# A sparse-attention stage whose two heads of a pair are normalised by one multiplication, with score buffers ordered by job

## What is computed

```
p_cmp = softmax(sc - slope * dist_c)
p_slc = softmax(ss - slope * dist_s)
p_win = softmax(sw - slope * dist_w)
o = gb[..., 0:1] * o_cmp + gb[..., 1:2] * o_slc + gb[..., 2:3] * o_win
```

## Time and profile before

| | |
|---|---|
| median of three runs | 3542.05 us (3542.04 to 3548.92) |
| the profiled execution | 3543.41 us |
| its span | 3541.6 us |
| the sparse attention's stretch in it | 1065.7 to 1337.0 us |

### The profile page before, as it was taken

One profiled execution on the slowest core, in us unless ns is written; L12 is line 12 of the kernel. 1 busy time (PEld: TensorE's weight loads), 2 busy tenths in 40 slices (PEclk: granted clock), 3 DMA queues, 4 the chain that ended last, 5 costly groups with the idle time before them and its releaser, 6 DMA issues.

```text
span 3541.6 us, 43801 instructions
## 1 busy us (share of the span) xinstructions
PE 3417.5 (96%) x16665; PEld 2705.3 (76%) x16665; DVE 1998.2 (56%) x4683; ACT 708.1 (20%) x1739; POOL 83.3 (2%) x104
## 2 busy tenths in 40 slices
PE   8999999999999999999998989999999999999988
PEld 3487688888655678888887767888887888887766
DVE  4473476544305667765456568543464667557566
ACT  2221021100114441211001153022112011131143
POOL 0000000000000000000000100000000000000100
PEclk9999999999999999999999999999999999999999
DMA  3202212222311112122221311212211222102311
GB/s 144 95 25 84 83 48 84 95 83 84 119 36 37 49 49 84 48 90 90 84 88 67 102 42 48 84 60 84 72 58 59 99 74 84 37 25 96 102 42 48
DMA packets 40120, 255.16 MB, mean 72 GB/s; under 512 B 5812, under 2 KB 5940, under 8 KB 11632
## 3 DMA queue, kind: packets, MB, share of 16 engines
q1 hardware_dynamic: 31616, 224.41, 17.8%
q0 software_dynamic: 3808, 16.12, 1.3%
q10 hardware_dynamic: 4496, 11.89, 1.2%
HBM read 243.73 MB, written 2.18 MB: 69 GB/s over the span
## 4 chain that ended last, share of the span: by engine, by line
PE 89%; DVE 8%; issue 1%; ACT 1%; DMA 1%; ACTq 0%; POOL 0%; POOLq 0%; DVEq 0%
PE PL L1194 27%; PE PX L1194 20%; PE PL L884 14%; PE PL L1535 4%; PE PL L1382 3%; PE PX L1644 2%; DVE SCR L2965 2%; PE PL L863 1%; PE PL L860 1%; PE PL L1298 1%; PE PX L1318 1%; DVE SCR L2980 1%; PE PL L1560 1%; PE PL L1347 1%; PE PX L894 1%
## 5 line engine op out<-in xcount | busy, mean ns | idle before, releaser
L884 PE MATMUL PL<-xn,ring 128*128 128x264 f32 (+1 forms) x1600 | 501.4, 471 | 11.6 <-DVE xn L2338 11.1
L884 PEld LDWEIGHTS PL<-xn,ring 128*128 128x128 f32 x1600 | 304.1, 192 | 193.9 <-issue 162.2
L1194 PE MATMUL PL<-Z,ring 128*128 128x256 f32 (+1 forms) x1344 | 318.1, 387 | 10.4 <-DVE Z L3355 8.6
L1194 PEld LDWEIGHTS PL<-Z,ring 128*128 128x128 f32 x1344 | 258.8, 193 | 52.3 <-DVE Z L3355 9.7
L1194 PE MATMUL PL<-AUX,ring 128*128 128x256 f32 (+1 forms) x1088 | 251.5, 379 | 0.0
L2381 DVE TENSOR_TENSOR Z<-PL,SCR 128x512 f32<-128x512 f32 (+1 forms) x72 | 50.2, 698 | 352.1 <-PE PL L884 337.2
L1194 PEld LDWEIGHTS PL<-AUX,ring 128*128 128x128 f32 x1088 | 206.6, 190 | 28.5 <-DVE AUX L2701 0.2
L1194 PE MATMUL PL<-xn,ring 128*128 128x264 f32 (+1 forms) x736 | 174.5, 389 | 12.7 <-DVE xn L2338 11.5
L1194 PE MATMUL PX<-Z,AUX 128*128 128x264 f32 (+1 forms) x768 | 178.3, 383 | 2.7 <-DVE Z L3163 2.7
L1194 PEld LDWEIGHTS PL<-xn,ring 128*128 128x128 f32 x736 | 141.1, 192 | 38.1 <-issue 10.9
L1813 ACT ACTIVATE SCR<-PL 128x256 f32<-128x256 f32 (+1 forms) x72 | 27.6, 383 | 698.7 <-PE PL L1194 698.7
(11 more groups left out here) (520 smaller groups left out, 5965.3 us busy)
## 6 DMA issues: line engine op xcount, KB each, us to landing
ring<-w_tiles SPq DMA_DIRECT2D x212, 1024.0 KB, 4.8
Z<-Z ACTq DMA_DIRECT2D x16, 264.0 KB, 4.7
SCR<-head_rows POOLq DMA_DIRECT2D x16, 264.0 KB, 3.8
AUX<-norm_scratch POOLq DMA_DIRECT2D x8, 528.0 KB, 6.5
Z<-mem POOLq DMA_DIRECT2D x3, 1024.0 KB, 11.0
cst<-consts ACTq DMA_DIRECT2D x1, 2188.5 KB, 15.9
resid<-x ACTq DMA_DIRECT2D x4, 512.0 KB, 9.6
Z<-norm_scratch POOLq DMA_DIRECT2D x4, 512.0 KB, 8.1
```

The costliest lines, as they stand in the source:

```text
L884: mm = pe.matmul(PL[:, 2 * h + c, 0:e - a], ring[t % 2][:, k, P * h:P * h + P], src_block(name, k)[:, a:e], start=k == 0, stop=k == KB - 1)
L1194: mm = pe.matmul(ps, lhs(k), rhs(k), start=kc == 0 and k == 0, stop=kc == per - 1 and k == 3)
```

## The change

The score buffers are counted by job, not by entry of the list: job number m has buffer m % 4 and the small columns of that buffer, so that the two heads of a pair lie in buffers 0 and 1, or 2 and 3. The compressed scores get columns of their own (5280 to 5536 of the scratch tile). At the first head of a pair normalise returns at once. At the second head it waits for that head's exponentials and does both heads: one reciprocal of the two sums, one product with the two gates, and one multiplication of both heads' columns by the two factors, spread along the columns. That raises na_nrm by two. The waits of the other functions are as before.

```
+        def nsa_scores(n):
+            return SCR[:, 5280:5536] if NSA[n][0] == "cmp" else Sbuf[NSA_JOB[n] % 4]
...
-                            mm = pe.transpose(pt_bank[n % 2][:, P * j:P * j + P], Sbuf[n % N_S][:, P * j:P * j + P], ident)
+                            mm = pe.transpose(pt_bank[n % 2][:, P * j:P * j + P], nsa_scores(n)[:, P * j:P * j + P], ident)
...
-                    act.activation(S, S, ACT.Exp, scale=-1.0, bias=nm[n % N_S], accum_out=sm[n % N_S]).then_inc(na_exp, 1)
+                    act.activation(S, S, ACT.Exp, scale=-1.0, bias=nm[m], accum_out=sm[m]).then_inc(na_exp, 1)
...
                 def normalise(n):
-                    S = Sbuf[n % N_S]
+                    if NSA[n][0] == "job" and NSA[n][3] == 0:
+                        return
+                    S = nsa_scores(n)
                     dve.wait_ge(na_exp, n + 1)
...
                     _, pr, i, e, br = NSA[n]
-                    at = 3 * (2 * pr + e) + 1 + br
-                    step(dve.reciprocal(rc[n % N_S], sm[n % N_S]))
-                    S = S[:, 0:P * (i + 1)]
-                    dve.tensor_scalar(S, S, rc[n % N_S], gates[:, i, at:at + 1], ALU.mult, ALU.mult).then_inc(na_nrm, 1)
+                    at, w, m = 6 * pr + 1 + br, P * (i + 1), NSA_JOB[n - 1] % 4
+                    total, scale = (tiny[:, c + 8 * m:c + 8 * m + 9:8] for c in (250, 252))
+                    step(dve.reciprocal(scale, total))
+                    step(dve.tensor_tensor(scale, scale, gates[:, i, at:at + 4:3], ALU.mult))
+                    both = SCR[:, 512 * m:512 * m + 1024].rearrange("p (e k) -> p e k", e=2)[:, :, 0:w]
+                    dve.tensor_tensor(both, both, scale.rearrange("p (e n) -> p e n", n=1).broadcast_to([P, 2, w]),
+                                      ALU.mult).then_inc(na_nrm, 2)
```

More of the change, by code:

```diff
@@ L1326, in turn @@
                         for i in range(4):
-                            mm = pe.transpose(pt_bank[n % 2][0:64, P * i:P * i + P], Sbuf[n % N_S][:, 64 * i:64 * i + 64], ident)
+                            mm = pe.transpose(pt_bank[n % 2][0:64, P * i:P * i + P], nsa_scores(n)[:, 64 * i:64 * i + 64], ident)
                     else:
                         for j in range(NSA[n][2] + 1):
-                            mm = pe.transpose(pt_bank[n % 2][:, P * j:P * j + P], Sbuf[n % N_S][:, P * j:P * j + P], ident)
+                            mm = pe.transpose(pt_bank[n % 2][:, P * j:P * j + P], nsa_scores(n)[:, P * j:P * j + P], ident)
                     mm.then_inc(na_tps, 1)
@@ L2027, in exps @@
                 def exps(n):
-                    S = Sbuf[n % N_S]
+                    S, m = nsa_scores(n), NSA_JOB[n] % 4
                     act.wait_ge(na_max, n + 1)
@@ L2674, in highest @@
                     dve.tensor_tensor_reduce(S[:, 0:w], head_tab[(2 * pr + e) % 4][:, 384 - P * i:512], sc_bank[n % 3][:, 0:w],
-                                             -0.125, 3e38, ALU.add, ALU.min, nm[n % N_S]).then_inc(na_max, 1)
+                                             -0.125, 3e38, ALU.add, ALU.min, nm[NSA_JOB[n] % 4]).then_inc(na_max, 1)
                 def normalise(n):
-                    S = Sbuf[n % N_S]
+                    if NSA[n][0] == "job" and NSA[n][3] == 0:
+                        return
+                    S = nsa_scores(n)
                     dve.wait_ge(na_exp, n + 1)
```

## The result

The changed kernel takes 3555.59 us (median of 7 runs, 3553.39 to 3556.66) against 3543.40 us for the kernel before in the same runs: a ratio of 1.0031, 95% interval 1.0022 to 1.0041. It is 12.2 us slower. The forecast was 9.4 us slower, at 3551.5 us, and the range up to 3558 holds the result.

What follows compares the result with a forecast made beforehand. TensorE was taken to bound the kernel, busy 96% of the span. Turns 7.9, score waits 1.0 and one evacuation 0.5 sum to 9.4 us, giving 3551.5 us from the 3542.05 median; range 3544 to 3558.

Steps and rivals of the forecast that it cites:

- The mechanism: Sparse attention stage: 19 turns without a projection in front end later; the other 45, covered by about 2 us, cost nothing.
- VectorE's saved work: Scaling of the pairs: 77.5 us removed, 73.6 us added, so VectorE saves 3.9 us, off TensorE's path.
- The tightest covered turn: Turn behind a projection with the least slack: first transpose at 1286.71, keeping 0.95 us after the later multiplication.
- The term of the turns: The 19 turns with no projection in front: 2.2, 1.7, 1.0 and 3.0 us by kind, together 7.9 us.
- (0.165 + 0.035) plus the difference of the multiplications: A pair's multiplication on VectorE ends later by gate product, step and multiplication difference: 0.28 to 0.87 us for 128 to 512 keys.
- the loop through ScalarE's copy and exponential: Rival, chance 0.13: a late multiplication delays turn, copy, next exponential and next multiplication; 3556 to 3560 us.
- The term of the score waits: TensorE's score matmuls waiting for reductions, in the 19 passes: +1.0 us, bounds -6.0 and +6.0.
- The rival that ended on the other side: Rival, chance 0.09: score waits shrink as first head's scaling leaves the queue; 3536.0 us, or 3532.2 with VectorE's saving.
- The rival of an absorbed lateness: Rival, chance 0.22: part of each lateness meets time TensorE already lost at the turns; half the sum, 3546.8 us.
- The rule: Judge TensorE by weight loads, 172.07 us against VectorE's 175.03 in the stage, making VectorE the engine to relieve.
- the marks named beforehand: Profile signs: VectorE some 4 us less busy, TensorE's busy time same, stage about 280.7 us, 15 to 19 turn waits.

Runs made afterwards that it cites:

- the kernel with those pairs alone: Changed kernel with one multiplication per pair only for the 45 pairs with a projection in front, the other 19 scaled head by head: 3544.96 us, ratio 1.0001.
- the buffers alone: Score buffers by job number, but each head scaled by itself as in the kernel before: 3543.95 us against 3543.93, ratio 1.0000.
- the two scalings: Changed kernel with the pair's one multiplication replaced by two, one per head, at the same place, each releasing its own turn: 3547.73 us, ratio 1.0009.
- the second product: Changed kernel plus a second small product of the factors that changes nothing, 0.20 us later for each of 64 pairs: 3557.40 us.
- the filler: Changed kernel with 3 to 6 identity transposes ahead of each of the 19 turns without a projection in front: 3554.00 us.
- the last one: Heads scaled one by one, 66 even projection shares, share after the turns in seven passes, distance tables made earlier: 3538.42 us against 3544.28, ratio 0.9984.

## Why the prediction was right, and where its sizes were off

**The mechanism** was the forecast's: the lateness of a pair's multiplication costs at turns with no projection in front, and no other turn waits for it. That the 45 covered turns cost nothing is shown by the kernel with those pairs alone; that buffers and addresses cost nothing, by the buffers alone; that VectorE's saved work is worth nothing, by the two scalings, which save more of it. The tightest covered turn of the earlier trace rows is here:

```profile
1291.10 1.23 DVE L2702 TENSOR_TENSOR SCR<-SCR,tiny 128x1024 f32<-128x1024 f32 x1
...
1293.39 0.60 PE L1334 MATMUL PL<-cst,SCR 128*128 128x128 f32 x4
```

The multiplication ends at 1292.33 and the first transpose starts at 1293.39: 1.06 us are left, against the 0.95 reckoned. After the change it is not the tightest; that is this one, of four blocks too, with 0.57 us:

```profile
1317.45 1.23 DVE L2702 TENSOR_TENSOR SCR<-SCR,tiny 128x1024 f32<-128x1024 f32 x1
...
1319.25 0.60 PE L1334 MATMUL PX<-cst,SCR 128*128 128x128 f32 x4
```

**The term of the turns** was 7.9 us and measured 9.9. The step "(0.165 + 0.035) plus the difference of the multiplications" took 0.035 us from one dependent instruction to the next. In the turn of the earlier trace rows, after the change:

```profile
1102.87 0.17 DVE L2699 RECIPROCAL tiny<-tiny 128x2 f32<-128x2 f32 x1 [0.34 <-ACT SCR L2038]
1103.07 0.16 DVE L2700 TENSOR_TENSOR tiny<-tiny,AUX 128x2 f32<-128x2 f32 x1
...
1103.34 0.69 DVE L2702 TENSOR_TENSOR SCR<-SCR,tiny 128x512 f32<-128x512 f32 x1
...
1104.08 0.44 PE L1334 MATMUL PX<-cst,SCR 128*128 128x128 f32 x2 [0.79 <-DVE SCR L2702]
...
1104.36 0.38 PE L1334 MATMUL PL<-cst,SCR 128*128 128x128 f32 x2
```

the reciprocal and the product follow each other in 0.20 us, but from the product's end (1103.23) to the multiplication it is 0.11 us. That is 0.07 us more than was reckoned, 16 times: 1.1 us. Neither the product ahead nor a spread operand makes the difference alone: in the kernel before, the product for the compressed scores (L2686) is followed by such a multiplication (L2687) with 0.3 us idle over 8, 0.04 each, and with two scalings at the pair's place the first follows the product in 0.035 us (0.6 us over the 16 first ones in each row above). What does was not tried. From the multiplication's end at 1104.03 to the two turns it is 0.05 and 0.33 us, against 0.28 reckoned for the second: 0.05 more, 16 times 0.8 us. The two together are 1.9 us, about what the term was short of.

The last turn of the stage is 1.06 us later, against 0.70 reckoned, but that is the clock and not the turn. Its first transposes, in the changed kernel and then in the one with the second product:

```profile
1345.09 0.69 PE L1334 MATMUL PX<-cst,SCR 128*128 128x128 f32 x2 [0.93 <-DVE SCR L2702]
```

```profile
1348.32 0.44 PE L1334 MATMUL PX<-cst,SCR 128*128 128x128 f32 x2 [1.13 <-DVE SCR L2703]
```

At the full clock this step is 0.31 us shorter, and with the second product's own 0.20 taken off it is 0.75. So the loop through ScalarE's copy and exponential, a rival in the prediction, added no more than 0.05 us even there.

**The term of the score waits** was +1.0 and measured -1.4. The prediction gave it bounds on both sides and chose the wrong sign: it looked at the 19 passes without a projection, and what got shorter are covered ones, in which no turn is later (read from the order, as said above, with the first head's scaling out of the way of the reductions). The rival that ended on the other side was right in this much, and its size was small.

**What was left out** is the clock: 3.1 us in the stage, and some of the 1.5 us behind it. The prediction read the full granted clock of the earlier trace rows as a constant, though its own sum took TensorE's idle time in the stage from 9 to 18 us. The Trainium skill, TensorE: Matmul & The Clock Gate, section "Part 1: The HAM clock gate (the "warmup" mystery)", says that the clock is set by how busy the array has been of late. The two falls, after 1.54 of 3.20 and 1.89 of 3.30 us, agree with that; the full clock after 1.54 of 3.20 with the filler, and after 1.88 of 3.30 with the second product, shows that the activity of these stretches alone does not decide it.

**Luck.** The score waits came out 2.4 us better than the sum had them and the clock 3.1 us worse, and neither was foreseen; without the first the total would have been 2.4 us further from the forecast. Of the 4.1 us between 3551.5 and 3555.59, 1.4 is the kernel before itself, 3543.40 us in these runs and 3542.05 on record.

**The rival of an absorbed lateness** is out: at 15 of the 18 turns that wait the second product's 0.20 us showed in full, and at the others more, or as much once the clock is taken off. **The rule** quoted for the rival on the other side (the Trainium skill, Perfetto Trace Analysis, "Identifying the Most-Contended Engine"), that VectorE is the engine to relieve when it is as busy as the weight loads, does not hold in this stage: VectorE's busy time fell by 8.6 us in one kernel here, and the stage grew.

Of the marks named beforehand, two did not come: VectorE's instructions do add up to 3.5 us less, but its busy time did not fall (176.8 us in the stage), as the instructions of a pair wait for each other where those of two heads overlapped; and TensorE's busy time rose with the half-clock stretches.

## What to carry to other kernels

Fusing two small operations into one delays the first result to the end of both; before doing it, list for each consumer what it has to do in between, and price only those with nothing. VectorE had idle time here, so less work for it gained nothing, and later results lost. Where cover is missing in some passes and plentiful in others, spread it evenly first: it made the change free here, and with two further edits a kernel 0.16% faster than before.

## What the runs showed of the hardware

A wait of some 1 us in a dense stage can cost more than itself. At 1204.66 the projection waits 1.22 us, and its eight matmuls then take 3.27 us at 1.2 GHz instead of the 1.99 of the same eight one pass earlier:

```profile
1199.65 1.99 PE L864 MATMUL PL<-Z,ring 128*128 128x256 f32 x8
...
1204.66 3.27 PE L864 MATMUL PL<-Z,ring 128*128 128x256 f32 x8 [1.22 <-DVE Z L2400]
```

It need not: in the kernel with the filler the same matmuls, after the same wait, run at the full clock.

```profile
1204.61 1.97 PE L866 MATMUL PL<-Z,ring 128*128 128x256 f32 x8 [1.22 <-DVE Z L2407]
```

So the 1.3 us between the two is the price of the half clock on these eight matmuls, and the wait alone does not tell whether it falls due.

And a later half-clock stretch, which every version has, is not equally long in all of them: behind the stage the span is 2204.1 to 2205.0 us in the four kernels whose stretch there lasts 17.1 us (before, buffers alone, second product, the last one) and 2205.6 to 2206.8 in the others, whose stretch lasts 20.5. What sets the one or the other I did not try; it means that differences of 2 us between two versions of this program need the trace of the stage beside the total.
